# 32 bytes ahead of the split activations and 32 behind them: where two tiles of a prompt-and-sample transformer layer start in the on-chip memory

## The reference

```python
def trunk_layer(x, c, attend, conv_buf, h0, lp):
    ada = jax.nn.silu(c) @ lp['w_ada'] + lp['b_ada']
    sh1, sc1, g1, sh2, sc2, g2 = [a[:, None, :] for a in jnp.split(ada, 6, axis=-1)]
    mix, states = mixer(x * (1 + sc1) + sh1, attend, conv_buf, h0, lp)
    x = layer_norm(ALPHA * x + (1 + g1) * mix, lp['ln_g'][0], lp['ln_b'][0])
    gt, up = jnp.split((x * (1 + sc2) + sh2) @ lp['w_ffn_in'], 2, axis=-1)
    f = (jax.nn.silu(gt) * up) @ lp['w_ffn_out']
    x = layer_norm(ALPHA * x + (1 + g2) * f, lp['ln_g'][1], lp['ln_b'][1])
    return x, states
```

## The kernel before, in words

| tiles | start before | by 64 | by 128 |
|---|---|---|---|
| `raw`; `whi0`, `whi1`, `wlo0`, `wlo1` | 16,512; 49,280 and on by 8,192 | 0 | 0 |
| `xhi`; `xlo` | 82,048; 100,480 | 0 | 0 |
| `ada` | 118,912 | 0 | 0 |
| `z` | 128,224 | 32 | 96 |
| `hhi`; `hlo` | 160,096; 185,440 | 32 | 96 |
| `ohi`; `olo`; `yhi`; `ylo` | 177,504; 186,720; 195,936; 205,152 | 32 | 96 |
| `wxhi0`, `wxlo0` and the other two pairs | 160,096 and on by 8,192 | 32 | 96 |

## Time and profile before

### The profile page before, as it was taken

One profiled execution on the slowest core, in us unless ns is written; L12 is line 12 of the kernel. 1 busy time (PEld: TensorE's weight loads), 2 busy tenths in 40 slices (PEclk: granted clock), 3 DMA queues, 4 the chain that ended last, 5 costly groups with the idle time before them and its releaser, 6 DMA issues.

```text
span 1777.5 us, 34633 instructions
## 1 busy us (share of the span) xinstructions
PE 1741.4 (98%) x13610; PEld 1607.3 (90%) x13610; DVE 899.4 (51%) x1632; ACT 710.7 (40%) x1076; POOL 156.7 (9%) x271
## 2 busy tenths in 40 slices
PE   8989999999999999999999999999999999999997
PEld 3558879888999999889988899999999999999997
DVE  2233346655656555555874344444444444444565
ACT  2223227764445443343563343333333333333334
POOL 0001312213322311100000000000000000000001
PEclk9999999999999999999999999999999999999998
DMA  9998878866655647985647764444455454544552
GB/s 354 380 380 308 295 245 296 286 213 236 200 178 171 205 148 278 334 315 193 200 142 264 284 223 165 159 135 163 162 185 185 157 167 160 167 151 142 166 164 85
DMA packets 114152, 384.06 MB, mean 216 GB/s; under 512 B 14941, under 2 KB 15325, under 8 KB 113662
## 3 DMA queue, kind: packets, MB, share of 16 engines
q1 hardware_dynamic: 103248, 349.82, 56.9%
q0 software_dynamic: 10208, 32.32, 5.6%
q10 hardware_dynamic: 590, 0.44, 0.1%
HBM read 373.48 MB, written 9.03 MB: 215 GB/s over the span
## 4 chain that ended last, share of the span: by engine, by line
PE 90%; DMA 5%; ACT 1%; DVE 1%; issue 1%; SPq 0%; POOL 0%; POOLq 0%; ACTq 0%; DVEq 0%
PE bank L714 26%; PE bank L716 25%; PE bank L715 25%; DMA raw<-in_w_units 5%; PE bank L721 3%; PE bank L761 3%; PE bank L739 2%; PE bank L887 1%; PE bank L1010 1%; DVE wlo L377 1%; PE bank L923 1%; DMA mgate<-mg 0%; SPq L478 0%; ACT z L1511 0%; PE bank L954 0%
## 5 line engine op out<-in xcount | busy, mean ns | idle before, releaser
L714 PE MATMUL bank<-xhi,wlo 128*128 128x288 f32 x2544 | 758.5, 298 | 2.4 <-DVE wlo L377 1.7
L715 PE MATMUL bank<-xlo,whi 128*128 128x288 f32 x2544 | 750.5, 295 | 0.0
L716 PE MATMUL bank<-xhi,whi 128*128 128x288 f32 x2544 | 748.1, 294 | 0.0
L377 DVE TENSOR_TENSOR wlo<-raw,whi 128x1024 fp32r<-128x1024 f32 (+2 forms) x468 | 510.0, 1127 | 380.5 <-ACT whi L369 373.3
L369 ACT CAST whi<-raw 128x1024 fp32r<-128x1024 f32 (+2 forms) x468 | 434.2, 969 | 421.1 <-PE bank L716 273.4
L714 PEld LDWEIGHTS bank<-xhi,wlo 128*128 128x128 f32 x2544 | 476.7, 187 | 15.7 <-issue 13.8
L716 PEld LDWEIGHTS bank<-xhi,whi 128*128 128x128 f32 x2544 | 479.1, 188 | 0.0
L715 PEld LDWEIGHTS bank<-xlo,whi 128*128 128x128 f32 x2544 | 477.7, 188 | 0.6
L716 PE MATMUL bank<-hhi,whi 128*128 128x288 f32 x704 | 208.7, 296 | 0.0
L714 PE MATMUL bank<-hhi,wlo 128*128 128x288 f32 x704 | 208.3, 296 | 0.0
L715 PE MATMUL bank<-hlo,whi 128*128 128x288 f32 x704 | 205.3, 292 | 0.0
(11 more groups left out here) (332 smaller groups left out, 1686.7 us busy)
## 6 DMA issues: line engine op xcount, KB each, us to landing
raw<-in_w_units SPq DMA_DIRECT2D x556, 512.0 KB, 6.1
raw<-in_w_ffn_out_units SPq DMA_DIRECT2D x64, 384.0 KB, 3.0
raw<-in_w_ffn_out_units SPq DMA_DIRECT2D x64, 320.0 KB, 3.4
raw<-in_w_units SPq DMA_DIRECT2D x16, 448.0 KB, 8.5
mgate<-mg POOLq DMA_DIRECT2D x32, 144.0 KB, 3.9
mgl<-mgate POOLq DMA_DIRECT2D x16, 288.0 KB, 7.0
bz<-relrow POOLq DMA_DIRECT2D x16, 192.0 KB, 3.5
xt<-in_x SPq DMA_DIRECT2D x8, 288.0 KB, 7.3
```

What stands on the lines that cost most here:

```text
L377: nc.vector.tensor_tensor(wlo[e][:, part], raw[:, s, spot], f32(whi[e][:, part]), ALU.subtract).then_inc(raw_used[s][h], 1)
L714: pe.matmul(acc, wt[1][:, w], x[0][:, c, :], start=start, stop=False)
L715: pe.matmul(acc, wt[0][:, w], x[1][:, c, :], start=False, stop=False)
L716: return pe.matmul(acc, wt[0][:, w], x[0][:, c, :], start=False, stop=stop)
```

## The change

Two tiles of 8 words are declared that nothing uses, one ahead of `xhi` and one behind `xlo`. `xhi` then starts at 82,080 and `xlo` at 100,512, both 32 bytes off a multiple of 64; all that is declared behind them starts 64 bytes later than before. `raw` and the weight tiles `whi`, `wlo` stay where they were. No instruction is added, removed or reordered.

```diff
         raw = sbuf(ctx, "raw", [P, RAW_SLOTS, UNIT])
         whi = [sbuf(ctx, f"whi{e}", [P, UNIT], F32R) for e in range(2)]
         wlo = [sbuf(ctx, f"wlo{e}", [P, UNIT], F32R) for e in range(2)]
+        sbuf(ctx, "gap0", [P, 8])
         xhi = sbuf(ctx, "xhi", [P, DC, T], F32R)
         xlo = sbuf(ctx, "xlo", [P, DC, T], F32R)
+        sbuf(ctx, "gap1", [P, 8])
 
         ada = sbuf(ctx, "ada", [P, NADA, NSEQ])
```

## The result

The changed kernel takes 1791.64 us, the median of 6 runs (1787.61 to 1796.29), the kernel before 1778.68 (1776.35 to 1779.82, 6 runs); the ratio is 1.0062 with a 95% interval of 1.0047 to 1.0077. The change makes the kernel slower by 0.6%, where the prediction had it faster by 0.46%. Its rival "the distance between the two operands by 128", with a chance of 0.14, had priced 1792 us. The profiled execution was the shortest of the six: span 1785.8 us, 8.3 over the span before, while the medians differ by 13.0.

The account below looks back on a forecast made before the run. TensorE's matmul rate was taken as the bound; 2436 triples x 3.35 ns = 8.2 us saved, other terms 0, giving 1769.3 us by the trace, 1769.7 on the median's scale (0.46% less); range 1765 to 1780, its own 1767 to 1773.

Parts of the forecast that it names:

- What bounds the kernel: TensorE's rate of starting 288-column matmuls bounds the time: busy 98% of the span, 90% of the chain.
- The front gap: Moving `xhi`, `xlo` by 32 bytes gives 396.65 instead of 400.0 ns a triple; 2436 x 3.35 = 8.2 us saved.
- The prediction's own sign: Sign to look for in the trace afterwards: if `hhi` goes over 400 ns, the rest by 128 is the cause.
- The back gap: Tiles behind move 64 bytes and keep their rest by 64: no cost; rest by 128 goes from 96 to 32.
- The `wx` triples: 80 triples with `wx` weights, both operands 32 off afterwards: between 396.65 and 403.3 ns, -0.5 us to 0, taken as 0.
- The splits: ACT's and DVE's 33 writes each into `xhi` and `xlo`: 33 x 2 ns, under 0.1 us, counted as nothing.
- the queries: First queries, 144 triples of L721 on `xhi`/`xlo`: bound 0.5 us either way, taken as 0.
- what is late next: A 16-triple unit goes from 6.4 to 6.35 us; DVE's and ACT's splits don't become the bound; total 1769.7 us.
- Slower by the distance: Rival: activations less weights by 128 counts; +8.0, +4.7 and +1.6 us on `xhi`, `hhi` and 256 more triples, 1792 us; chance 0.14.
- its rule: The slower rival decides from the point where a triple in the steady stages takes over 400.0 ns.
- Nothing moves: Rival: tiles' distance within the partition causes the rates, so 32 bytes change nothing: 0 us, 1777.9 us; chance 0.12.
- the deeper gain: Rival: shifted stream falls into the early groups' 131.4 ns rhythm, saving 5.7 ns a triple, 13.9 us, 1764 us; chance 0.03.

## Why the prediction was wrong

The measured distances, with the steady time of a triple (whole weight loads; w, x are the rests by 128 of weights and activations):

| distance | ns | seen with w, x |
|---|---|---|
| 0 | 400.0 | 0, 0; 32, 32; 96, 96 |
| 16 | 398.4 to 398.6 | 0, 16; 96, 112 |
| 32 | 403.3 or 400.0 | 0, 32; 96, 0 |
| 48 | 396.0 to 396.3 or 400.0 | 0, 48; 96, 16 |
| 64 | 396.7 | 0, 64; 96, 32 |
| 80 | 400.0 | 0, 80; 96, 48 |
| 96 | 396.7 (32, 0: 396.9) | 0, 96; 32, 0; 96, 64 |
| 112 | 395.0 or 400.0 | 0, 112; 96, 80 (395.0 alone) |
| 112 | 396.7 | 112, 96 |

**What bounds the kernel: right.** TensorE's rate is the time. 3.33 ns more on a triple came through undiminished in the steady stage: +2.34 us in 704 triples, and no engine or transfer took over.

**The front gap: the step that failed.** It said that the shift moves the blocks "into the class in which `hhi` is now. Price: 396.65 instead of 400.0". The class was by 64; what counts among the 32-byte steps is the distance to the weights by 128, and that of `xhi` became 32, not the 96 of `hhi`. Where the prediction had -3.35 ns a triple, the steady stages had +3.33. Rest 96, the class of `hhi`, did give -3.3 ns (1772.33 us). Not all of the +3.33 is the front gap's own: alone it left the steady stage at 400.0 ns, with `xhi` at the same distance of 32. Which of its two rhythms distance 32 falls into depends on something else, and on what is not shown. The prediction's own sign for this came true: `hhi` went over 400 ns. Both numbers had been read rightly, 96 off and 32 off were in the rows; I merged two rests that differ by 64 into one. The layout table had a column by 128 that told them apart.

**The back gap: failed too.** "By rest 64 that costs nothing": it moved `hhi` from distance 96 to 32, and the two FOUT stages cost 2.35 and 2.33 us, 4.7 in all, more than half of the profiled difference. Here too the other gap has a part: with the back gap alone the two stages cost 1.2 and 1.7 us. A gap that the change puts behind the tiles it means to move is a change of every tile behind it.

**The `wx` triples: within the bounds.** 400.0 ns for both operands at rest 32, about 3 ns less: under 0.2 us for the 48 triples of `step`.

**The splits, the queries, what is late next: right.** DVE's and ACT's splits stayed at 1127 and 969 ns, and the first stages moved by less than they scatter.

**The rivals.** Slower by the distance had its three terms at +8.0, +4.7 and +1.6 us. In the profiled execution they measured +7.5 (2.34 + 2.0 + 0.7 + 2.5), +4.7 and, as matmuls of CMB, +1.3, which the longer wait and the half clock in the trace of before hid. Its 1792 us met the median of 1791.64, and its rule held; that nearly all stages would stay at 403.3, where the front gap alone ran at 400.0, its rows couldn't tell, and so far the closeness is luck. The prediction held against it that the own start explains the three rows "with the smaller assumption", and that was the wrong weight: three rows that two rules fit equally leave the rules equal. "Nothing moves" and the deeper gain are out for this layout; a rate below 396.65 exists all the same, 395.0 at distance 112. The 131.4 ns that the deeper gain was priced by came from rounded rows: over all 312 starts within the groups of L721 the trace of before has 132.8 ns, 398.5 for three.

**Against the pages.** The Trainium skill (TensorE: Matmul & The Clock Gate, Step-by-step: what each phase is for) says that the weight load takes no read bandwidth from the running matmul. Whether bandwidth is what is taken no run here shows, but the two aren't independent: with `xhi` at rest 0 a triple takes 400.0 ns with the weights at 0, 403.3 at 96 and 396.9 at 32. The prediction's 122.5 ns is an estimate by the formula of that page's section on the back-to-back issue gap, which the section gives for an isolated gap and not for a stream with a weight load before each matmul; the traces have 131.7 to 134.4. The Trainium skill (SBUF — State Buffer, Specifications (TRN2)) gives lines of 16 bytes. The trace agrees that 16 bytes count, 398.6 ns at distance 16 against 400.0 at 0; that two whole lines change nothing, as the prediction drew from it, the runs refute, 403.3 at 32 and 396.7 at 64.

**What stays open.** Why a matmul of 288 columns takes 131.7 to 134.4 ns, and by what the distance acts; what decides which rhythm a stage catches; what drives the scatter of single runs, 8.7 us over six of the changed kernel and 9.1 over 29 of the kernel before, beyond the stretches at half clock that differ from trace to trace.

**The better version.** With both activation tiles at rest 64 every triple in the trace, `wx` included, is at 396.7 ns with no second rhythm seen in two profiles, and 1771.1 and 1771.5 us beat both kernels: 0.9948 and 0.9958 of before. The activations at 112 have the lowest median, 0.9941, but the intervals overlap and one profile showed two rates. I would take 64.

## What to carry to other kernels

When a trace holds the same instruction at two rates, write down the starts of all its operands, not of the one that differs most visibly, and test every modulus (64, 128) that tells the rows apart before putting a price on a shift. A gap moves all tiles behind it: pad it to a whole period, here 128 bytes (`hhi`, moved by 128 or 256, kept 396.7 ns in eight kernels), if only one tile is meant. Where thousands of matmuls follow each other without a wait, their distance to the weights is worth 0.4 to 0.6% here, and it costs a few bytes to try.

## What the runs showed that I had not expected

A stream of equal matmuls settles into a rhythm of several triples (133, 133, 134 ns at distance 0; triples of 400 and 407 in turn at distance 32), and one layout can hold two: 395.0 and 400.0 ns in the two halves of one execution, or 400.0 and 403.3 on the two sides of a short break. At half clock a triple takes 720 ns at distance 0 and at 96 alike. With half the weight columns and outputs the order of the distances turned, 393.3 ns at 32 against 395.0 at 0.
